# Output projection of the last block from single fp32 products to split halves (one Trainium2 core)

## The chip, the cores and the metric

One core of one Trainium2 chip runs the whole program. The metric is device time in microseconds (us) of one execution; lower is better. The time before is the median of three runs.

## The reference, cut to what matters

A two-layer first model (each layer: feed-forward, a mixing block, cross attention, feed-forward, each with a layer norm) is followed by one second-model block on 256 tokens of width 1024. The change is in that last block:

```python
y = sigmoid(ma) * ya + sigmoid(mb) * yb            # 256 x 1024, fp32
h = layer_norm_2(DEEPNORM_ALPHA * h + y @ w_out[i], ln1_g[i], ln1_b[i])
m = moe(h, w_router, b_router, w_up, b_up, w_down, b_down)   # 32 experts, top 4
h = layer_norm_2(DEEPNORM_ALPHA * h + m, ln2_g, ln2_b)
h = h + sigmoid(h @ w_ple_gate + b_ple_gate) * (p @ w_ple)
```

`ya` comes from a gated linear recurrence, `yb` from gated linear attention, normalised by the root of its mean square. `ma`, `mb` and the gates are projections of h. Only `y @ w_out` is computed in another way after the change.

## The kernel before, in words

**Weights.** SyncE (SP) loads weight tiles of 128 x 2048 fp32 (1 MB) into slots 0 to 5 of a ring of 12. A slot is free again when TensorE (PE) has counted the tile as used. Two forms of product exist. In the plain form PE multiplies fp32 by fp32; the trace then has two matmul records for one product. In the split form weight and activation are each the sum of two fp32r parts: high (ScalarE, ACT, copies with rounding, L1299 in `high`) and low (VectorE, DVE, subtracts, L1766 in `low`, written over the tile in its ring slot). PE then makes three fp32r products, high x high, high x low and low x high, one record each (`by_columns` L583 with 256 columns, `by_rows` L607, `rows_part` L596 and `tail` L645 with 512 columns). The high halves of weights take turns in ring slots 6 to 8; the halves of the activations lie in slots 9 (`xh`) and 10 (`xl`).

**Who splits when.** A list of tile names, `split_order` with `ORDER_MIX2` as its end, gives the order. `three_on(name)` is the tile three places later: `next_high(name)` on ACT (L1301) waits until `name` has been used by PE, which frees its high slot, and copies the tile three on; `next_low(name)` on DVE (L1769) subtracts for it. Where nothing is three on, neither does anything. Before the change the list ends with `ma3`, so the four tiles `w2o0` to `w2o3` of the output projection are not split.

**The end of the last block before the experts.** PE's order (L1002 on): `ga3`, `ma0`, `ma1` (split, by columns), sixteen matmuls with a matrix of ones for the mean squares (L1011, two banks, 0 and 1), then `ma2` in bank 0 and `ma3` in bank 1, then the output projection in the plain form: tile 0 for both halves t of the tokens, then tiles 1 to 3 for t = 0 and then for t = 1, with the eight transposes of the normed half t = 0 (L634) put before the last product group. ACT's order (L1651 on): sigmoid of `ma0`, `ma1` (L1643 in `through_r`, each followed by `next_high`), two square roots of the mean squares (L1405 in `roots`, they empty banks 0 and 1), sigmoids of `ma2` and `ma3`, a table load for the layer norm, the layer norm. DVE's order (L2154 on): low of `ma3`, gates `ma0`, `ma1` (L2132), two reciprocals (L2162), then for each j of 0 to 3 the part y_j: two products out of PSUM (L2166), one (L2173), for j of 2 and 3 the gate product (L2132), one addition (L2178). Then the layer norm (L1807).

**The experts.** Router, top 4, positions and gates follow the layer norm on PE, DVE and ACT (L1053 to L1089). SP starts to load expert 0 into all 12 slots as soon as `w2o3` is used (L541), as four pairs for the up projection and two pairs for the down projection; each later pair waits until PE has used the slots' former contents. Per expert PE gathers tokens (L1126), makes gate and up (L1154), transposes (L1167), combines (L1135) and makes the down product (L1192).

Of the kernel before, what the change touches and what calls it, by code (L numbers as in the profile page):

```python
# [16 lines left out]
F32 = mybir.dt.float32  # L17
F32R = mybir.dt.float32r
U8 = mybir.dt.uint8
ALU = mybir.AluOpType  # L20
# [3 lines left out]
P = 128  # L24
T = 256
TT = T // P
D = 1024
# [102 lines left out]
class Fork:  # L130
# [21 lines left out]
    def join(self):  # L152
        for ln, n in zip(self.lines, self.most):
# [3 lines left out]
ORDER_MIX1 = ("rq0", "rq1", "cc", "ch", "cb", "pu", "ri0", "ri1", "ck0", "ck1", "ck2", "ck3", "rg0", "rg1",  # L157
              "cv0", "cv1", "cv2", "cv3", "wo0", "wo1", "wo2", "wo3", "cq2", "cq3", "co0", "co1", "co2", "co3")
ORDER_MIX2 = ("xa2", "xa3", "q0", "q1", "k0", "k1", "v0", "v1", "v2", "v3", "go0", "go1", "go2", "go3",
              "mb0", "mb1", "mb2", "mb3", "ga0", "ga1", "ga2", "ga3", "ma0", "ma1", "ma2", "ma3")  # L160


def ffn_order(tag):
# [18 lines left out]
def program(nc, book, a):  # L182

    book.iters = {}
    with ExitStack() as ctx:
# [19 lines left out]
        hn = sb("hn", [P, TT, D])  # L205
# [20 lines left out]
        ps = ctx.enter_context(nc.psum_tensor("ps", [P, 8, 512], F32))  # L226
# [9 lines left out]
        dve_done = line("dve_done")  # L236
# [12 lines left out]
        slot_of = book.slots  # L249
# [15 lines left out]
        yT = w(Y, 2048, "p (g t) -> p g t", g=8)  # L265
# [3 lines left out]
        xh = ring_halves[XH][:].rearrange("p (k t) -> p k t", k=DT)  # L269
        xl = ring_halves[XL][:].rearrange("p (k t) -> p k t", k=DT)  # L270
# [287 lines left out]
        def _(pe):  # L558
# [5 lines left out]
            def open_bank(b, name):  # L564

                emptied[b].add(name)
                pe.wait_ge(emptied[b].sem, emptied[b].at(name))
# [4 lines left out]
            def arrived(name, plus=0):  # L572
                s = slot_of[name]
                pe.wait_ge(loaded[s].sem, loaded[s].at(name, plus))
                return s

            def release(mm, name):
                mm.then_inc(used[slot_of[name]].sem, 1)

            def full(mm, name):  # L580
                mm.then_inc(pe_full.add(name), 1)
# [46 lines left out]
            def transposes(tag, t, src):  # L628

                b = t_bank(tag, t)  # L630
                open_bank(b, ("T", tag, t))
                open_bank(b + 1, ("T", tag, t))
                for k in range(DT):
                    mm = pe.transpose(ps[:, b + k // 4, (k % 4) * P:(k % 4) * P + P], src[:, t, strip(tag, k)],  # L634
                                      ident[:])
                full(mm, ("T", tag, t))

            def normed(tag, t):
                pe.wait_ge(dve_done.sem, dve_done.at(("hn", tag, t)))
# [303 lines left out]
            s = arrived("glr")  # L943
            for k in range(DT):
                mm = pe.matmul(ps[0:16, 0, 0:T], ring[:, s, k * 16:k * 16 + 16], hT[:, k, :],
                               start=(k == 0), stop=(k == DT - 1))
# [25 lines left out]
            s = arrived("glg")  # L972
            for j in range(2):
                open_bank(2 + j, ("zg", j))
                for kk in range(2):
                    c0 = (2 * j + kk) * P
                    mm = pe.matmul(ps[:, 2 + j, kk * T:kk * T + T], ring[0:16, s, c0:c0 + P], work[0:16, FQ:FQ + T],
                                   start=True, stop=True)
# [35 lines left out]
            by_columns("ma2", 0)  # L1014
            by_columns("ma3", 1)

            def w2o_part(j, kk, t):
                s = slot_of[f"w2o{j}"]
                for half in range(2):
                    mm = pe.matmul(ps[:, 4 + 2 * t + half, :], yT[:, 2 * j + kk, t * P:t * P + P],  # L1020
                                   ring[:, s, kk * D + half * 512:kk * D + half * 512 + 512],
                                   start=(j == 0 and kk == 0), stop=(j == 3 and kk == 1))
                return mm

            def y_part(j):
                arrived(f"w2o{j}")
                pe.wait_ge(dve_done.sem, dve_done.at(("y", "g", j)))

            y_part(0)
            for t in range(TT):  # L1030
                open_bank(4 + 2 * t, "w2o")
                open_bank(5 + 2 * t, "w2o")
                for kk in range(2):
                    mm = w2o_part(0, kk, t)
            release(mm, "w2o0")
            after = ("A",)
            for j in (1, 2, 3):
                y_part(j)
                for kk in range(2):
                    mm = w2o_part(j, kk, 0)  # L1040
            full(mm, ("t0", after))
            for j in (1, 2, 3):
                for kk in range(2):
                    if (j, kk) == (3, 1):
                        normed(after, 0)
                        transposes(after, 0, hn)
                    mm = w2o_part(j, kk, 1)
                release(mm, f"w2o{j}")
            normed(after, 1)
            transposes(after, 1, hn)  # L1050
            turned_copied(after, 0)
# [226 lines left out]
        def _(act):  # L1278
# [50 lines left out]
            def root_table():  # L1329
                nc.scalar.activation(small[:, 61:62], epsc[:, 0:1], ACT.Sqrt)  # L1330
# [306 lines left out]
            def through_r(nm, j, fn):  # L1637
                slot_used(act, f"{nm}{j}")
                if j >= 2:
                    act.wait_ge(dve_done.sem, dve_done.at((nm, j - 2)))  # L1640
                elif nm == "ma":
                    act.wait_ge(dve_done.sem, dve_done.at(("ga", 2 + j)))
                nc.scalar.activation(work[:, R + 512 * (j % 2):R + 512 * (j % 2) + 512], ps[:, j % 2, :], fn)\  # L1643
                    .then_inc(emptied[j % 2].sem, 1)
                next_high(f"{nm}{j}")
# [7 lines left out]
            roots([("ms", "g", j) for j in range(2)], 256, 0)  # L1653
            through_r("ma", 2, ACT.Sigmoid)
            through_r("ma", 3, ACT.Sigmoid)
            root_table()
            ln(("A",), ("ln1_g_2", "ln1_b_2"), 0)

# [77 lines left out]
        def _(dve):  # L1736
# [3 lines left out]
            def done(ins, name):  # L1740
                ins.then_inc(dve_done.add(name), 1)
# [14 lines left out]
            def act_event(name):  # L1756
                dve.wait_ge(act_done.sem, act_done.at(name))
# [11 lines left out]
            def next_low(name):  # L1769
                ahead = three_on(name)  # L1770
                if ahead is not None:
                    low(ahead)
# [34 lines left out]
            def ln(tag, gname, i, alpha):  # L1807


                parts = tail_of(tag)  # L1810
                dve.wait_ge(h_ready.sem, h_ready.at(("h", before_ln(tag))))
                for t in range(TT):
                    if t == 0:
                        pe_group(("t0", tag))
                    else:
                        slot_used(dve, parts[2])
                    for half in range(2):
                        c = slice(half * 512, half * 512 + 512)
                        v.scalar_tensor_tensor(out=hn[:, t, c], in0=h[:, t, c], scalar=alpha,
                                               in1=ps[:, 4 + 2 * t + half, :], op0=ALU.mult, op1=ALU.add)\  # L1820
                            .then_inc(emptied[4 + 2 * t + half].sem, 1)
                    for half in range(2):
                        bank_empty(4 + 2 * t + half, acc_name(tag))
                        ins = v.bn_stats(stat[:, t, half, :], hn[:, t, half * 512:half * 512 + 512])
                    done(ins, ("stats", tag, t))
                    mine(("stats", tag, t))
                    normalise_rows(tag, t)
                    evac_T(tag, t, gname, i)
                    if tag[0] != "A":
                        x_low(tag, t)  # L1830
                if tag[0] != "A":
                    for name in parts:
                        next_low(name)
# [321 lines left out]
            for j in range(2):  # L2155
                mine(("ga", j))
                times("ma", j)

            dve.wait_ge(pool_done.sem, pool_done.at(("mb", 3)))
            for j in range(2):  # L2160
                bank_empty(j, ("ms", "g", j))
                link(v.reciprocal(work[:, Q + 512 * j:Q + 512 * j + 512], work[:, Q + 512 * j:Q + 512 * j + 512]))  # L2162
            for j in range(4):
                for uu in range(2):
                    u = 2 * j + uu
                    ins = v.scalar_tensor_tensor(out=work[:, FQ + u * T:FQ + u * T + T],  # L2166
                                                 in0=ps[:, obank("g", j), uu * T:uu * T + T],
                                                 scalar=col("gla_norm_g_2", uu), in1=work[:, Q + j * T:Q + j * T + T],
                                                 op0=ALU.mult, op1=ALU.mult)
                ins.then_inc(emptied[obank("g", j)].sem, 1)  # L2170
                bank_empty(obank("g", j), ("O", "g", j))
                x = work[:, FQ + 512 * j:FQ + 512 * j + 512]
                link(v.tensor_tensor(x, x, hn[:].rearrange("p t n -> p (t n)")[:, 512 * j:512 * j + 512], ALU.mult))  # L2173
                if j >= 2:
                    mine(("ga", j))
                    times("ma", j)
                mine(("ma", j))
                done(v.tensor_tensor(work[:, Y + 512 * j:Y + 512 * j + 512], x,  # L2178
                                     work[:, XC + 512 * j:XC + 512 * j + 512], ALU.add), ("y", "g", j))
            ln(("A",), ("ln1_g_2", "ln1_b_2"), 0, ALPHA2)  # L2180


# [304 lines left out]
```

## Time and profile before

| | |
|---|---|
| median of 3 runs | 2537.65 us (2536.61 to 2537.88) |
| the profiled execution's own time | 2539.67 us |
| its span, first to last instruction | 2537.9 us |
| PE busy | 2446.8 us (96%) |
| DVE busy | 1101.9 us (43%) |
| ACT busy | 827.2 us (33%) |
| POOL busy | 217.8 us (9%) |
| read from HBM | 662.50 MB, 261 GB/s over the span |
| mean granted TensorE clock | 0.982 |

All positions in the trace are microseconds from the first instruction. "Busy" adds up the time in which an engine has an instruction running. A timeline line is: start, duration, engine, line, operation, output <- inputs, how many were merged, and in brackets the idle time of the engine before it and what ended it. The end of a matmul is modelled and contains the way through the array, so the pace of a row of matmuls is read from start to start, not from the duration of one.

### The profile page before, as it was taken

What the parts mean: (1) busy time and instruction counts of PE and PEld (TensorE: products, weight loads), DVE (VectorE), ACT (ScalarE), POOL (GpSimd) and SP (SyncE); (2) the same over time, 40 slices, a digit from 0 to 9 for tenths busy, and PEclk for the clock granted to TensorE, in tenths of its full rate; (3) what the DMA queues carried; (4) which work ended last, traced back from release to release, by engine and by line L of the source; (5) the groups of instructions that cost most, each with busy time, mean ns of one, the idle gap of its engine ahead of it and who ended that gap; (6) DMA issues with size and microseconds to landing.
All of it is one profiled execution on the core that took longest, in us unless ns stands there. A gap on an engine that the chain in (4) does not pass through costs nothing. (4 is left out here: it accounts for less than half of the span.)

```text
span 2537.9 us, 36251 instructions
## 1 busy us (share of the span) xinstructions
PE 2446.8 (96%) x15029; PEld 1797.8 (71%) x15029; DVE 1101.9 (43%) x1411; ACT 827.2 (33%) x952; POOL 217.8 (9%) x101
## 2 busy tenths in 40 slices
PE   8999999999999999999999989999999999999977
PEld 8899988999999998899989944444444444444433
DVE  5457756644644867654569721112211111211122
ACT  4344344433433444443355411212221122212120
POOL 0002402200200432100111010000000000000001
PEclk9999999999999999999999979999999999999997
DMA  7565454565565545456455347999999999999980
GB/s 238 191 202 163 150 183 143 173 199 182 170 207 175 164 150 170 146 184 205 156 163 185 117 199 316 427 429 428 428 429 429 428 428 428 428 428 429 429 368 17
DMA packets 215307, 665.16 MB, mean 262 GB/s; under 512 B 9841, under 2 KB 164207, under 8 KB 190624
## 3 DMA queue, kind: packets, MB, share of 16 engines
q1 hardware_dynamic: 214912, 662.53, 68.4%
q8 instruction: 86, 1.41, 0.2%
q10 hardware_dynamic: 288, 1.05, 0.1%
q14 instruction: 21, 0.17, 0.0%
HBM read 662.50 MB, written 1.05 MB: 261 GB/s over the span
## 5 line engine op out<-in xcount | busy, mean ns | idle before, releaser
L592 PE MATMUL ps<-ring_halves 128*128 128x256 f32 x5984 | 757.4, 284 | 7.9 <-DVE ring_halves L1862 5.6
L592 PEld LDWEIGHTS ps<-ring_halves 128*128 128x128 f32 x5984 | 738.1, 193 | 12.0 <-DVE ring_halves L1862 6.0
L1766 DVE TENSOR_TENSOR ring_halves<-ring,ring_halves 128x2048 fp32r<-128x2048 f32 x206 | 516.0, 2513 | 367.7 <-ACT ring_halves L1299 367.5
L1299 ACT CAST ring_halves<-ring 128x2048 fp32r<-128x2048 f32 x206 | 391.3, 1903 | 280.9 <-PE ps L592 138.2
L1154 PE MATMUL ps<-ring,work 128*64 128x512 f32 x2048 | 452.8, 596 | 23.1 <-DMA ring<-in_w_up_dram 22.3
L1287 ACT COPY work<-ps 128x512 f32<-128x512 f32 x185 | 106.9, 587 | 844.8 <-PE ps L1154 391.5
L1154 PEld LDWEIGHTS ps<-ring,work 128*64 128x64 f32 x2048 | 145.8, 137 | 324.1 <-issue 269.4
L603 PE MATMUL ps<-ring_halves,work_halves 128*128 128x512 f32 x1184 | 288.5, 391 | 0.0
L2254 DVE TENSOR_SCALAR work<-work 128x128 f32<-128x128 f32 x64 | 19.3, 343 | 606.3 <-PE ps L1154 606.3
L2375 POOL TENSOR_TENSOR h<-hn,work 128x1024 f32<-128x1024 f32 x20 | 79.0, 3949 | 2106.8 <-DVE hn L1804 1066.9
L603 PEld LDWEIGHTS ps<-ring_halves,work_halves 128*128 128x128 f32 x1184 | 219.7, 188 | 44.4 <-issue 0.5
L1192 PE MATMUL ps<-ring,work 128*64 128x512 f32 x1024 | 226.8, 595 | 2.0
L1192 PEld LDWEIGHTS ps<-ring,work 128*64 128x64 f32 x1024 | 70.8, 137 | 137.5 <-issue 127.9
L603 PE MATMUL ps<-ring_halves 128*128 128x512 f32 x544 | 138.3, 393 | 1.3 <-ACT work L1287 1.3
L1126 PE MATMUL ps<-work,h 128*128 128x64 f32 x1056 | 132.8, 286 | 2.1 <-issue 2.1
L1126 PEld LDWEIGHTS ps<-work,h 128*128 128x128 f32 x1056 | 130.0, 200 | 3.6 <-issue 3.6
L673 PE MATMUL ps<-hT,ring 128*128 128x128 f32 x1024 | 118.1, 276 | 3.3 <-ACT hT L1317 3.3
L673 PEld LDWEIGHTS ps<-hT,ring 128*128 128x128 f32 x1024 | 116.2, 192 | 6.5 <-ACT hT L1317 6.5
L603 PEld LDWEIGHTS ps<-ring_halves 128*128 128x128 f32 x544 | 101.6, 188 | 23.6 <-issue 2.9
L2271 DVE TENSOR_TENSOR work<-work 128x256 f32<-128x256 f32 x64 | 27.2, 425 | 135.6 <-ACT work L1684 131.6
L1349 ACT ACTIVATE work<-ps 128x512 f32<-128x512 f32 x44 | 26.3, 597 | 140.2 <-PE ps L592 140.2
L1135 PE MATMUL ps<-work 64*128 64x512 f32 x264 | 65.6, 615 | 0.7 <-ACT work L1287 0.7
(260 smaller groups left out, 1744.3 us busy)
## 6 DMA issues: line engine op xcount, KB each, us to landing
ring<-in_w_up_dram SPq DMA_DIRECT2D x128, 2048.0 KB, 22.3
ring<-in_w_down_dram SPq DMA_DIRECT2D x64, 2048.0 KB, 19.4
ring<-in_w_in_dram SPq DMA_DIRECT2D x52, 1024.0 KB, 5.2
ring<-in_ffn_gate_dram SPq DMA_DIRECT2D x44, 1024.0 KB, 5.3
ring<-in_ffn_up_dram SPq DMA_DIRECT2D x44, 1024.0 KB, 5.3
ring<-in_ffn_down_dram SPq DMA_DIRECT2D x44, 1024.0 KB, 4.9
ring<-in_w_out_dram SPq DMA_DIRECT2D x12, 1024.0 KB, 4.9
ring<-in_ca_k_dram SPq DMA_DIRECT2D x8, 1024.0 KB, 5.1
```

The lines of the kernel that those rows point to most:

```text
L592: mm = pe.matmul(ps[:, bank, pt * T:pt * T + T], wt[:, o:o + P], x[:, k, :], start=(k == 0 and n == 0), stop=(k == DT - 1 and n == 2))
L603: mm = pe.matmul(ps[:, 4 + 2 * t + half, :], x, wt[:, o:o + 512], start=(start and n == 0), stop=(stop and n == 2))
L673: mm = pe.matmul(ps[:, bank, pt * T + t * P:pt * T + t * P + P], ring[:, slot_of[name], o:o + P], hT[:, k, t * P:t * P + P], start=(k == 0 ...
L1126: mm = pe.matmul(ps[:, 2, k * CAP:k * CAP + CAP], h[:, t, strip(("A",), k)], work[:, GS + t * CAP:GS + t * CAP + CAP], start=(t == 0), sto ...
L1135: mm = pe.matmul(ps[:, 4 + 2 * t + half, :], work[lo:lo + CAP, GGT + t * P:GGT + t * P + P], work[lo:lo + CAP, YS:YS + 512], start=False, ...
L1154: mm = pe.matmul(ps[lo:lo + CAP, x, :], work[:, XG + k * CAP:XG + k * CAP + CAP], ring[:, s, c0 + 512 * x:c0 + 512 * x + 512], start=(k == ...
L1192: mm = pe.matmul(ps[half * CAP:half * CAP + CAP, 3, :], work[:, ACTS + f * CAP:ACTS + f * CAP + CAP], ring[:, s, kk * D + half * 512:kk * ...
L1287: nc.scalar.copy(dst, ps[:, bank, :] if src is None else src).then_inc(emptied[bank].sem, 1)
L1299: nc.scalar.copy(high_of(name)[:], ring[:, s, :]).then_inc(hi_done.add(name), 1)
L1766: v.tensor_tensor(ring_halves[s][:], ring[:, s, :], high_of(name)[:].bitcast(F32), ALU.subtract)\
L2271: done(v.tensor_tensor(w(ACTS + 256 * x, 256), uh, w(SG + 256 * x, 256), ALU.mult), ("few", x))
L2375: link(g.tensor_tensor(h[:, t, :], hn[:, t, :], w(at, D), ALU.mult))
```

## The change

The names `w2o0` to `w2o3` are put at the end of the split list. That alone makes four existing calls do something they did not do: ACT's `next_high` behind the sigmoids of `ma1`, `ma2` and `ma3` now copies the high halves of `w2o0`, `w2o1` and `w2o2`. The copy behind `ma1` stands ahead of the two square roots in ACT's order. On DVE, `next_low` for `ma1`, `ma2` and `ma3` is called behind the parts y_1, y_2 and y_3. After the last sigmoid, ACT copies the four high parts of y into `xh` (which the gate projections have used until then), then the high half of `w2o3`, for which it waits until PE has used `w2o0`. DVE makes the four low parts of y behind the low half of `w2o2`, then the low half of `w2o3`. PE's hand-written projection is replaced by `by_rows` and `tail`, in the same order of tiles and token halves.

```diff
-              "mb0", "mb1", "mb2", "mb3", "ga0", "ga1", "ga2", "ga3", "ma0", "ma1", "ma2", "ma3")
+              "mb0", "mb1", "mb2", "mb3", "ga0", "ga1", "ga2", "ga3", "ma0", "ma1", "ma2", "ma3", "w2o0", "w2o1", "w2o2", "w2o3")
...
-            y_part(0)
-            for t in range(TT):
-                open_bank(4 + 2 * t, "w2o")
-                open_bank(5 + 2 * t, "w2o")
-                for kk in range(2):
-                    mm = w2o_part(0, kk, t)
-            release(mm, "w2o0")
+            def y_ready(j):
+                pe.wait_ge(dve_done.sem, dve_done.at(("ylow", "g", j)))
+
             after = ("A",)
-            for j in (1, 2, 3):
-                y_part(j)
-                for kk in range(2):
-                    mm = w2o_part(j, kk, 0)
-            full(mm, ("t0", after))
-            for j in (1, 2, 3):
-                for kk in range(2):
-                    if (j, kk) == (3, 1):
-                        normed(after, 0)
-                        transposes(after, 0, hn)
-                    mm = w2o_part(j, kk, 1)
-                release(mm, f"w2o{j}")
+            y_ready(0)
+            by_rows("w2o0", halves(0), start=True, opening="w2o")
+            tail(after, [(f"w2o{j}", halves(2 * j), lambda j=j: y_ready(j)) for j in (1, 2, 3)])
...
             through_r("ma", 2, ACT.Sigmoid)
             through_r("ma", 3, ACT.Sigmoid)
+            for j in range(4):
+                act.wait_ge(dve_done.sem, dve_done.at(("y", "g", j)))
+                done(nc.scalar.copy(xh[:, 2 * j:2 * j + 2, :], yT[:, 2 * j:2 * j + 2, :]), ("yhigh", "g", j))
+            next_high("w2o0")
             root_table()
...
+            def y_low(i):
+                act_event(("yhigh", "g", i))
+                done(v.tensor_tensor(xl[:, 2 * i:2 * i + 2, :], yT[:, 2 * i:2 * i + 2, :],
+                                     xh[:, 2 * i:2 * i + 2, :].bitcast(F32), ALU.subtract), ("ylow", "g", i))
...
                                      work[:, XC + 512 * j:XC + 512 * j + 512], ALU.add), ("y", "g", j))
+                if j:
+                    next_low(f"ma{j}")
+            for j in range(4):
+                y_low(j)
+            next_low("w2o0")
             ln(("A",), ("ln1_g_2", "ln1_b_2"), 0, ALPHA2)
```

## Rows read from the trace of the kernel before

**Rows 1.** The page, the span in 40 equal slices: bandwidth.
```profile
GB/s 238 191 202 163 150 183 143 173 199 182 170 207 175 164 150 170 146 184 205 156 163 185 117 199 316 427 429 428 428 429 429 428 428 428 428 428 429 429 368 17
```

**Rows 2.** Timeline of PE around the output projection.
```profile
1444.63 11.86 PE L592 MATMUL ps<-ring_halves 128*128 128x256 f32 x96
1459.50 27.68 PE L1020 MATMUL ps<-ring,work 128*128 128x512 f32 x60 [3.01 <-DVE work L2166]
1487.02 1.10 PE L634 MATMUL ps<-ident,hn 128*128 128x128 f32 x8
1487.96 1.88 PE L1020 MATMUL ps<-ring,work 128*128 128x512 f32 x4
```

**Rows 3.** Busy time, clock and DMA by stretch.
```profile
core 0: us, PE busy (x) PEld busy (x) DVE busy (x) ACT busy (x) POOL busy (x), PEclk, DMA share, GB/s
1456.50:1459.50 3.00, 0.00 (x1) 0.03 (x1) 2.90 (x6) 2.08 (x3) 0.00 (x0) 1.00 0.00 0
1459.50:1463.80 4.30, 4.30 (x6) 1.80 (x7) 1.96 (x3) 0.00 (x0) 0.00 (x0) 0.60 0.00 0
1489.80:1494.00 4.20, 0.04 (x1) 0.00 (x0) 3.67 (x7) 0.29 (x1) 0.00 (x0) 1.00 0.62 187
1494.00:1520.00 26.00, 20.99 (x68) 14.87 (x68) 5.43 (x30) 4.63 (x9) 4.69 (x2) 0.51 1.01 430
1529.30:1536.10 6.80, 6.80 (x18) 2.00 (x20) 0.00 (x0) 1.13 (x1) 0.00 (x0) 0.56 0.01 2
1700.00:2400.00 700.00, 678.20 (x3508) 299.02 (x3506) 128.39 (x384) 144.10 (x216) 0.00 (x0) 1.00 1.01 429
```

**Rows 4.** Timeline of SP, the loads of expert 1 into the up slots.
```profile
1536.13 10.63 SPq L370 DMA_DIRECT2D ring<-in_w_up_dram  x4
```

**Rows 5.** Timeline of PE, gate and up of expert 0 and expert 1.
```profile
1529.26 16.91 PE L1154 MATMUL ps<-ring,work 128*64 128x512 f32 x64 [0.75 <-ACT work L1287]
...
1560.40 13.90 PE L1154 MATMUL ps<-ring,work 128*64 128x512 f32 x64
```

**Rows 6.** Timeline of ACT ahead of the output projection.
```profile
1430.54 1.89 ACT L1299 CAST ring_halves<-ring 128x2048 fp32r<-128x2048 f32 x1
1432.45 1.28 ACT L1643 ACT_TABLE_LOAD   x1
...
1441.56 0.60 ACT L1643 ACTIVATE work<-ps 128x512 f32<-128x512 f32 x1 [3.37 <-PE ps L592]
1442.18 1.28 ACT L1405 ACT_TABLE_LOAD   x1
...
1443.47 0.69 ACT L1405 ACTIVATE work<-ps,epsc 128x512 f32<-128x512 f32 x1
```

**Rows 7.** Timeline of DVE ahead of the output projection, and the norm of its first half.
```profile
1432.46 2.29 DVE L1766 TENSOR_TENSOR ring_halves<-ring,ring_halves 128x2048 fp32r<-128x2048 f32 x1 [8.22 <-ACT ring_halves L1299]
1434.67 0.69 DVE L2132 TENSOR_TENSOR work<-work 128x512 f32<-128x512 f32 x1
...
1444.26 6.74 DVE L2162 RECIPROCAL work<-work 128x512 f32<-128x512 f32 x2 [1.31 <-ACT work L1405]
...
1451.04 0.87 DVE L2166 SCALAR_TENSOR_TENSOR work<-ps,cols,work 128x256 f32<-128x256 f32 x2
...
1460.84 0.69 DVE L2178 TENSOR_TENSOR work<-work 128x512 f32<-128x512 f32 x1
...
1482.00 0.81 DVE L1804 TENSOR_SCALAR hn<-hn,mv,rstd 128x1024 f32<-128x1024 f32 x1
```

**Rows 8.** Timeline of DVE in an earlier layer, the low half of 512 columns.
```profile
608.85 0.69 DVE L1847 TENSOR_TENSOR work_halves<-work,work_halves 128x512 fp32r<-128x512 f32 x1
```

**Rows 9.** Timeline of PE, 24 split products of 512 columns and what follows.
```profile
468.67 5.63 PE L603 MATMUL ps<-ring_halves,work_halves 128*128 128x512 f32 x24
474.13 11.68 PE L592 MATMUL ps<-ring_halves 128*128 128x256 f32 x96
```

**Rows 10.** Timeline of PE, 96 products of 256 columns after a longer idle time.
```profile
82.59 14.15 PE L592 MATMUL ps<-ring_halves 128*128 128x256 f32 x96 [5.61 <-DVE ring_halves L1862]
```

More of the change, by code:

```diff
@@ L1015, in _ @@
             by_columns("ma3", 1)
[L1017 to L1027, printed above, removed]
-            y_part(0)
-            for t in range(TT):
-                open_bank(4 + 2 * t, "w2o")
-                open_bank(5 + 2 * t, "w2o")
-                for kk in range(2):
-                    mm = w2o_part(0, kk, t)
-            release(mm, "w2o0")
-            after = ("A",)
-            for j in (1, 2, 3):
-                y_part(j)
-                for kk in range(2):
-                    mm = w2o_part(j, kk, 0)
-            full(mm, ("t0", after))
-            for j in (1, 2, 3):
-                for kk in range(2):
-                    if (j, kk) == (3, 1):
-                        normed(after, 0)
-                        transposes(after, 0, hn)
-                    mm = w2o_part(j, kk, 1)
-                release(mm, f"w2o{j}")
+            def y_ready(j):
+                pe.wait_ge(dve_done.sem, dve_done.at(("ylow", "g", j)))
+            after = ("A",)
+            y_ready(0)
+            by_rows("w2o0", halves(0), start=True, opening="w2o")
+            tail(after, [(f"w2o{j}", halves(2 * j), lambda j=j: y_ready(j)) for j in (1, 2, 3)])
             normed(after, 1)
```

## The prediction, made before the changed kernel was run

> **What bounds the kernel now.** I read the page's 40 slices first. From slice 25 on the bandwidth stands at 428 to 429 GB/s, while before that it wanders around 180 [rows 1]. So there are two regimes: PE sets the time up to the experts, and the experts run at the pace of their weight loads. The stretch table says the same: from 1700 to 2400 us the DMA share is 1.01, and PE has 22 us free in 700 [rows 3]. The reader has to see what joins the regimes. The twelve slots hold just one expert, and the loads of expert 1 start when PE has used the first pair of expert 0, at 1536.13 [rows 4], 6.9 us after its gate and up products began at 1529.26 [rows 5]. From there the stream is full, so the end of the kernel moves one to one with that moment, and that moment hangs on PE's chain through projection, layer norm and router. No slack in the experts absorbs a shift: a stream that starts later ends later.
>
> Next I read the timelines around the projection, one engine at a time. PE ends `ma3` at about 1456.5 and begins the projection at 1459.50, after 3.0 us of idle time; it ends at 1487.96 + 1.88 = 1489.84, so it takes 30.3 us [rows 2]. In those 3.0 us DVE is busy for 2.90 [rows 3]: from the reciprocals at 1444.26 to the last addition at 1460.84 DVE works without a break [rows 7]. PE is quick to be held up here because DVE is the engine that is late. That is what the change has to be weighed against: it relieves PE and adds work to DVE.
>
> **What it takes from PE.** The plain projection is 64 records, 30.3 us with its transposes. The new one has 4 tiles x 2 row blocks x 2 token halves x 2 column halves x 3 = 96 products. A block of 24 such products has its successor start 474.13 - 468.67 = 5.46 us after it, 0.2275 us each [rows 9]; 96 make 21.8 us. With the transposes at 1487.96 - 1487.02 = 0.9 us [rows 2] and 0.2 us for the way out of the last product this is 22.9 us at full clock. 30.3 - 22.9 = 7.4 us would be the gain if both ran under the same clock.
>
> They do not. After 3.0 us of idle time the clock was 0.60 of full in the first 4.3 us [rows 3], a loss of 1.7 us that lies within the 30.3. After an idle time of 5.61 us, 96 products took 14.15 us [rows 10], where 96 of the same kind at full clock took 11.86 [rows 2]: 2.3 us lost. The new idle time will be 12.8 us (below), for which no row stands; the bounds are 1.7 (the row after 3.0 us) and 3.4 (twice that), and I take 2.3, the row with the longer idle time. The new projection then takes 25.2 us, which is 5.1 less than now.
>
> The rows of plain products give another possible pace: 60 records from 1459.50 to 1487.02, less the 1.7 us, are 0.43 us each [rows 2, 3]. If a record is two passes, a pass of 512 columns takes 0.215 us, and 96 take 20.6 us, 1.2 us less than by rows 9. I keep rows 9, because they are the same instruction in the same helper. The Trainium skill (TensorE: Matmul & The Clock Gate, Back-to-back issue gap) gives 216 ns for an isolated product of 512 columns, by which the sum would be 1.1 us smaller. The same section gives some 131 ns for sustained pairs of weight load and product; that would be 12.6 us and turn the sum to a gain of about 3 us (estimates from the page). The trace disagrees with both, by its 0.2275 us.
>
> **What it puts on the path.** I follow it instruction by instruction.
>
> (a) ACT, behind the sigmoid of `ma1` at 1441.56: the copy of `w2o0` (slot free, tile landed) would start 0.5 us later and push the table load from 1442.18 to 1443.96, since a table load follows such a copy by 1432.45 - 1430.54 = 1.91 us. The square root moves from 1443.47 to 1445.25, by 1.8 us [rows 6]. Two things wait for it. PE wants bank 0 for `ma2`: it began at 1444.63 [rows 2] and now begins at about 1446.1, so `ma3` ends at 1457.9 instead of 1456.5; this 1.4 us hides behind (b). DVE wants the root: its chain moves from 1444.26 to 1446.0 [rows 7]. Only this second wait counts.
>
> (b) DVE, three low halves of weights between and behind the parts of y: each takes 2.29 us and holds the next instruction back by 1434.67 - 1432.46 = 2.21 [rows 7], so 6.6 us. Their high halves are done by then (copies behind the sigmoids of `ma1`, `ma2`, `ma3`, the last at about 1460.4, wanted at 1467.7). Nothing else runs on DVE that could cover them.
>
> (c) DVE, the low half of y_0: 0.69 us [rows 8]. The copies of y on ACT run while DVE works and cost nothing; if that cover were gone, the one in front of PE would cost another 0.6 us, the length of ACT's instruction on 512 columns [rows 6].
>
> So PE may start after the last addition, which lets a successor go at 1461.5 [rows 7], plus 1.8, plus 6.6, plus 0.7, plus 0.1 for the event: 1470.7 instead of 1459.5. **PE starts 11.2 us later**, after 12.8 us of idle time. It can't start on y_0 earlier, although y_0 is ready long before, because DVE makes all low parts behind y_3.
>
> (d) `w2o3`: its high half waits for PE to use `w2o0`, 24 products into the projection. Copy 1.9 and subtraction 2.3 with two events make 4.4 us; PE has the 24 products of `w2o1` and `w2o2` for t = 0 in the meantime, 5.5 us. It fits by 1.1 us, so 0.
>
> (e) Layer norm: the last product of t = 0 is PE's 40th record now, at about 1459.5 + 40 x 0.43 + 1.7 = 1478.4, and DVE has normed that half at 1482.00 + 0.81 = 1482.8 [rows 7], 4.4 us later; PE will have 30 products, 6.8 us, in that time, so 0. SP's order is unchanged; expert 0's loads start later with `w2o3`, need some 30 us and have as long as before. POOL does nothing here.
>
> **The sum.** 11.2 later, 5.1 shorter: +6.1 us at the layer norm, and through the router to 1536.13 unchanged in length. The clock there adds luck. Expert 0's first products had a clock of 0.56 [rows 3], and all 64 took 16.91 where expert 1's took 13.90 [rows 5]: 3.0 us are lost, and where the clock rises relative to the work can be better for the changed kernel by up to 1.7, or worse by a little. I take 0.2 off for it: +5.9. The working is in the profiled execution, which took 2539.67 us by its own time, 2.0 above the median; this execution would become 2545.6. Against the median of 2537.65 I forecast **2543.6 us**. About 0.2%, 5.1 us, is what a measurement can tell from no change.
>
> **The rivals.**
>
> *The shift stays under 5.1 us (within 0.2%), 0.27.* Either the root isn't pushed (table load or copy elsewhere in ACT's queue): then +4.1, 2541.8. Or the pace is 0.215: +4.7, 2542.4. Or the clock rises earlier at expert 0 than now: +4.2. For it speaks that the forecast lies only 0.8 us above the border; against the first that ACT runs in order in every row, against the second rows 9.
>
> *`w2o3` is late, or the clock stays low longer, 0.10.* The margin in (d) is 1.1 us, and the upper bound of the clock's loss costs 1.1 more than I took. A stall of 1 to 2 us on top makes +7 to +9, 2545 to 2547.
>
> *Faster: the clock stays up through the router, 0.04.* Place: the gap of 4.2 us after the projection. In it the clock was 1.00, and in the 26 us behind it 0.51, with PE busy for 21.0 [rows 3]. Should the clock stay at full there, at most half of the 21.0 would go, 10.5 us, and 3.0 at expert 0. It decides from 5.9 us saved; with all 13.5 the time is 2537.65 + 5.9 - 13.5 = 2530. Against it: the gap before and the waits within the stretch are as they were, and the change touches neither. The short pace of the page's sustained figure would end here too; it is counted in the 0.04.
>
> *The change doesn't do what it says* is no rival here: the four names enter the split list, and both engines' helpers follow that list.
>
> **How the numbers follow.** Forecast 0.59 with its own range of +5.1 to +7.3; under the border 0.27; later still 0.10; faster 0.04. For eight in ten I take +3.1 to +8.9: 2540.7 to 2546.5, which leaves out the faster case, the lowest tip of the second and the highest of the third. Slower by over 0.2%: 0.59 + 0.10 = 0.69; within: 0.27; faster: 0.04.
>
> **What would show it.** Right: root L1405 at about 1445.3; three subtractions L1766 of 2.29 us between 1457 and 1470; PE idle for 12 to 13 us before the first L603 product and reading DVE as its releaser; 96 products in 24 to 26 us with the transposes; SP's second batch of up loads at about 1542. Wrong: PE's first product before 1469 or after 1472, a gap on PE in front of `w2o3`, products at another pace than 0.2275 us, or a stretch from layer norm to experts that changes its length by over 2 us.

## The result, and the profile after

The changed kernel takes 2542.75 us (median of 16 runs, 2539.82 to 2546.17) against 2537.81 us before (16 runs, 2535.88 to 2541.45): 4.9 us more, ratio 1.002 with a 95% interval of 1.0012 to 1.0027, which is +3.0 to +6.9 us. The forecast was 2543.6 us, +5.9. Its profiled execution took 2543.03 us, span 2541.2.

The timeline of PE after, around the projection, the mean-square products (L1011) as its first row. Columns as in [rows 2].

```profile
1440.75 3.61 PE L1011 MATMUL ps<-work,ones 128*128 128x256 f32 x16
1445.38 11.77 PE L592 MATMUL ps<-ring_halves 128*128 128x256 f32 x96 [1.02 <-ACT work L1380]
1469.96 23.57 PE L603 MATMUL ps<-ring_halves 128*128 128x512 f32 x90 [12.81 <-DVE ring_halves L2140]
1493.38 1.11 PE L634 MATMUL ps<-ident,hn 128*128 128x128 f32 x8
1494.24 1.64 PE L603 MATMUL ps<-ring_halves 128*128 128x512 f32 x6
```

PE now waits 12.81 us where it waited 3.01 [rows 2], and its releaser is DVE's low part of y (L2140). A new, small gap of 1.02 us stands in front of `ma2` (second row), released by ACT's square root. The projection lasts from 1469.96 to 1495.88, 25.9 us, where it lasted 30.3.

The timeline of ACT after, which answers to [rows 6]:

```profile
1440.94 0.60 ACT L1618 ACTIVATE work<-ps 128x512 f32<-128x512 f32 x1 [3.37 <-PE ps L592]
1441.44 1.89 ACT L1274 CAST ring_halves<-ring 128x2048 fp32r<-128x2048 f32 x1
1443.35 1.28 ACT L1380 ACT_TABLE_LOAD   x1
1444.64 1.27 ACT L1380 ACTIVATE work<-ps,epsc 128x512 f32<-128x512 f32 x2
...
1478.61 1.91 ACT L1274 CAST ring_halves<-ring 128x2048 fp32r<-128x2048 f32 x1 [10.85 <-PE ps L603]
```

The copy stands between sigmoid and table load, and the root begins 3.70 us behind the sigmoid; before it was 1443.47 - 1441.56 = 1.91. The last row is the copy of `w2o3`, which waited for PE to use `w2o0`.

The timeline of DVE after, which answers to [rows 7]. The rows left out are instructions of y_0 to y_3.

```profile
1445.43 6.74 DVE L2146 RECIPROCAL work<-work 128x512 f32<-128x512 f32 x2 [3.09 <-ACT work L1380]
1452.20 0.88 DVE L2150 SCALAR_TENSOR_TENSOR work<-ps,cols,work 128x256 f32<-128x256 f32 x2
...
1456.69 2.28 DVE L1745 TENSOR_TENSOR ring_halves<-ring,ring_halves 128x2048 fp32r<-128x2048 f32 x1
...
1461.86 2.28 DVE L1745 TENSOR_TENSOR ring_halves<-ring,ring_halves 128x2048 fp32r<-128x2048 f32 x1
...
1466.41 0.69 DVE L2162 TENSOR_TENSOR work<-work 128x512 f32<-128x512 f32 x1
1467.02 2.28 DVE L1745 TENSOR_TENSOR ring_halves<-ring,ring_halves 128x2048 fp32r<-128x2048 f32 x1
1469.22 2.49 DVE L2140 TENSOR_TENSOR ring_halves<-work,ring_halves 128x512 fp32r<-128x512 f32 x4
1480.55 2.29 DVE L1745 TENSOR_TENSOR ring_halves<-ring,ring_halves 128x2048 fp32r<-128x2048 f32 x1 [8.84 <-ACT ring_halves L1274]
```

From 1445.43 to 1471.7 there is no idle time on DVE, with three low halves in between. The last row is the low half of `w2o3`: done at 1482.8. PE is busy for 19.88 of the 19.90 us in question (next fence), so it was in time.

Stretches of the kernel after, columns as in [rows 3]: the gap, the first 6 us of the projection, and the rest of it.

```profile
1457.20:1469.90 12.70, 0.00 (x0) 0.00 (x0) 12.50 (x15) 4.64 (x6) 0.00 (x0) 0.57 0.00 0
1470.00:1476.00 6.00, 6.00 (x14) 4.80 (x15) 1.71 (x3) 0.00 (x0) 0.00 (x0) 0.50 0.00 0
1476.00:1495.90 19.90, 19.88 (x91) 16.21 (x90) 7.33 (x12) 5.07 (x8) 4.73 (x2) 1.00 0.00 1
```

DVE is busy for 12.50 of the 12.70 us in which PE does nothing, and PE starts at a clock of 0.50.

SP after, the loads of expert 0 and the first of expert 1, which answers to [rows 4]:

```profile
1496.40 2.46 SPq L370 DMA_DIRECT2D ring<-in_w_up_dram  x4
...
1541.99 10.63 SPq L370 DMA_DIRECT2D ring<-in_w_up_dram  x4
```

**One ruler for all traces.** Executions differ by up to 2.5 us in what comes before. So the text below counts positions from the start of the mean-square products (L1011), whose operands the change doesn't touch; the fences keep the time from the first instruction. That start is at 1441.37 in the first trace of before and at 1440.75 after. The first output product comes at 18.1 before and 29.2 after, the load of expert 1 at 94.8 and 101.2.

### The profile page after: what moved, and what is told of

Its sections match the earlier page's. It is cut to its first block and busy times, and to the rows that moved or that the text cites. A ratio compares the mean times of both kernels' runs of the same rounds, so it can differ in the third digit from the quotient of the medians.

```text
span 2541.2 us, 36335 instructions
## 1 busy us (share of the span) xinstructions
PE 2441.4 (96%) x15061; PEld 1804.6 (71%) x15061; DVE 1113.5 (44%) x1419; ACT 836.7 (33%) x960; POOL 218.0 (9%) x101
## 5 line engine op out<-in xcount | busy, mean ns | idle before, releaser
L592 PEld LDWEIGHTS ps<-ring_halves 128*128 128x128 f32 x5984 | 737.8, 193 | 13.4 <-DVE ring_halves L1841 5.8
L1745 DVE TENSOR_TENSOR ring_halves<-ring,ring_halves 128x2048 fp32r<-128x2048 f32 x210 | 525.1, 2509 | 376.3 <-ACT ring_halves L1274 376.1
L1274 ACT CAST ring_halves<-ring 128x2048 fp32r<-128x2048 f32 x210 | 398.8, 1903 | 292.0 <-PE ps L592 138.2
L1129 PE MATMUL ps<-ring,work 128*64 128x512 f32 x2048 | 452.8, 596 | 23.1 <-DMA ring<-in_w_up_dram 22.3
L1129 PEld LDWEIGHTS ps<-ring,work 128*64 128x64 f32 x2048 | 145.6, 137 | 324.3 <-issue 269.4
L603 PE MATMUL ps<-ring_halves 128*128 128x512 f32 x640 | 163.5, 398 | 14.1 <-DVE ring_halves L2140 12.8
L603 PEld LDWEIGHTS ps<-ring_halves 128*128 128x128 f32 x640 | 121.7, 191 | 40.9 <-DVE ring_halves L2140 13.0
```

Source lines behind the costliest of these rows:

```text
L592: mm = pe.matmul(ps[:, bank, pt * T:pt * T + T], wt[:, o:o + P], x[:, k, :], start=(k == 0 and n == 0), stop=(k == DT - 1 and n == 2))
L603: mm = pe.matmul(ps[:, 4 + 2 * t + half, :], x, wt[:, o:o + 512], start=(start and n == 0), stop=(stop and n == 2))
L1129: mm = pe.matmul(ps[lo:lo + CAP, x, :], work[:, XG + k * CAP:XG + k * CAP + CAP], ring[:, s, c0 + 512 * x:c0 + 512 * x + 512], start=(k == ...
L1274: nc.scalar.copy(high_of(name)[:], ring[:, s, :]).then_inc(hi_done.add(name), 1)
L1745: v.tensor_tensor(ring_halves[s][:], ring[:, s, :], high_of(name)[:].bitcast(F32), ALU.subtract)\
```

## The experiments

The theory: PE's start is the end of DVE's chain, every low half on it costs its 2.2 us, ACT's early copy 1.8 us, and the products save what their pace says, less the clock. Rival A: PE waits for ACT's copies, not for DVE. Rival B: the loss is a matter of the clock and of luck behind the projection. The intervals below are those of the difference to the kernel before in runs on the same chip.

**1. ACT's roots first.**

```diff
-            def through_r(nm, j, fn):
+            def through_r(nm, j, fn, ahead=True):
...
-                next_high(f"{nm}{j}")
+                if ahead:
+                    next_high(f"{nm}{j}")
...
-            through_r("ma", 1, ACT.Sigmoid)
+            through_r("ma", 1, ACT.Sigmoid, ahead=False)
             roots([("ms", "g", j) for j in range(2)], 256, 0)
+            next_high("ma1")
```

> Edit: the changed kernel with one thing undone, the copy of w2o0's high half stands behind the two square roots on ACT. Theory (DVE's chain sets PE's start): roots, reciprocals and all that follows on DVE move 1.8 us earlier, PE's gate projections 1.4 us earlier, so PE's idle time before the first output product goes from 12.8 to about 12.4 us and the time falls by 1.8 us against the changed kernel (2542.75), to +3.1 against the kernel before. Rival A (PE waits for ACT's high halves, not for DVE): this puts the copy of w2o0 later by 2 us, PE starts later or no earlier, time +4.9 to +7. Rival B (the loss is phase of the clock and luck behind the projection): no change, +4.9.

```profile
1442.39 3.61 PE L1011 MATMUL ps<-work,ones 128*128 128x256 f32 x16
1445.65 11.86 PE L592 MATMUL ps<-ring_halves 128*128 128x256 f32 x96
1469.82 22.33 PE L603 MATMUL ps<-ring_halves 128*128 128x512 f32 x90 [12.31 <-DVE ring_halves L2142]
```

The fence is the PE timeline of this kernel. The gap before `ma2` is gone, the idle time is 12.31, and the first output product comes at 27.4, which is 1.8 earlier. The time is 2541.74 (11 runs) against 2538.01 of the kernel before on the same chip: +3.7, interval +0.5 to +5.1. Rival A wanted PE to start no earlier, and falls. Rival B wanted +4.9, which the interval of the runs doesn't exclude; this experiment leaves it to the next one.

**2. DVE's parts of y first.**

```diff
-                if j:
-                    next_low(f"ma{j}")
             for j in range(4):
                 y_low(j)
-            next_low("w2o0")
+                next_low(("ma1", "ma2", "ma3", "w2o0")[j])
```

> Edit: the changed kernel, with DVE's order changed only: all four parts of y first, then low of y_0, low of w2o0, low of y_1, low of w2o1 and so on. No work is removed. Theory: two lows of 2.2 us leave the path to PE's first product, idle time 12.8 - 4.4 = 8.4 us, time 4.4 us under the changed kernel, +0.5 against the kernel before. Rival A (ACT is what PE waits for): idle time stays 12.8, +4.9. Rival B (clock and luck): the idle time falls, but the time stays within 2 us of the changed kernel's.

```profile
1442.28 3.61 PE L1011 MATMUL ps<-work,ones 128*128 128x256 f32 x16
...
1467.14 22.16 PE L603 MATMUL ps<-ring_halves 128*128 128x512 f32 x90 [8.45 <-DVE ring_halves L1745]
```

In this PE timeline the start is at 24.9, 4.35 earlier, and the idle time is 8.45. The releaser is now L1745, the low half of `w2o0`. The same work in another order brings the time to 2536.85 (11 runs), -1.2 against before, interval -3.0 to +1.8: no difference that can be told. That is 6.1 under the changed kernel's +4.9, more than the theory's 4.4. At the load of expert 1 it is 6.2 earlier (94.65 against a mean of 100.86): 4.35 come from the start; 1.2 come from a projection of 24.5 us against 25.9 and 25.4, and 0.7 from behind the projection, both by an earlier rise of the clock (last section). Rival A wanted an idle time of 12.8 us and rival B a time within 2 us of the changed kernel's; both fall, though a part of the 6.1 is the clock.

**3. Both.** The two edits together.

> Edit: both of the former, ACT's roots first and DVE's parts first. Theory: the two add up, PE idle 12.4 - 4.4 = 8.0 us, 6.2 us under the changed kernel, -1.3 against the kernel before (2536.5). Rival B: within 2 us of the changed kernel.

The first output product comes at 23.1 (1464.67, mean-square products from 1441.59), 6.1 earlier than in the changed kernel; idle time 7.96. The time is 2538.06 (11 runs), 0.0 against before, interval -3.3 to +1.3. The start was as forecast; the total was forecast 1.3 lower, inside the interval.

**4. Low halves of the weights cut short.**

```diff
-                v.tensor_tensor(ring_halves[s][:], ring[:, s, :], high_of(name)[:].bitcast(F32), ALU.subtract)\
+                n = 8 if name in ("w2o0", "w2o1", "w2o2", "w2o3") else SLOT
+                v.tensor_tensor(ring_halves[s][:, 0:n], ring[:, s, 0:n], high_of(name)[:, 0:n].bitcast(F32), ALU.subtract)\
...
+                if name in ("w2o0", "w2o1", "w2o2", "w2o3"):
+                    low = high
```

> Edit: the changed kernel, with the low halves of the four w2o tiles cut to 8 of 2048 columns on DVE; PE multiplies by the high half once more in place of the low one, so the number and kind of its products is the same. Leaves out: the low half of w_out in the product, so the output is that of a rounded w_out. Theory: three subtractions of 2.2 us become about 0.1 us each, PE idle 12.8 - 6.3 = 6.5 us, 6.3 us under the changed kernel, -1.4 against the kernel before. Rival A (ACT): PE's start is then held by the last copy of y_0 or of w2o0 and moves by under 2 us. Rival B: within 2 us of the changed kernel.

The expectation is wrong on the output: the high product enters twice where the low one is missing, so the projection comes out far from that of a rounded `w_out`. The products on PE keep their number and kind. The three subtractions in front of PE's start last 0.16 us each. The first output product comes at 22.8 (1463.30, mean-square products from 1440.46), 6.4 earlier than in the changed kernel, after 6.43 us of idle time. The time is 2536.35 (11 runs), -1.7 against before, interval -3.8 to +0.8. So the three subtractions are 6.4 of the 11.1 us that PE starts late.

**5. PE kept busy in the gap.**

```diff
+            pe.wait_ge(emptied[6].sem, emptied[6].at("w2o"))
+            pe.wait_ge(pool_done.sem, pool_done.at(("mb", 3)))
+            for _ in range(12):
+                pe.matmul(ps[:, 6, :], ones[:], hn[:, 0, 0:512], start=True, stop=True)
             y_ready(0)
```

> Edit: the changed kernel, with 12 fp32 products of 512 columns (ones by the gated values, into a bank that the projection opens later and overwrites) put on PE between ma3 and the wait for y_0's low part. They take 10.3 us of the 12.8 us of idle time. Theory: they keep the clock at full, and the projection takes 23.0 us instead of 25.9 from first product to last; PE's start does not move; 2.9 us under the changed kernel, +2.0 against the kernel before. Rival (the 25.9 us are the products' own pace behind a wait, not the clock): the projection stays at 25.9 us and the time at +4.9.

```profile
1442.70 3.61 PE L1011 MATMUL ps<-work,ones 128*128 128x256 f32 x16
...
1458.95 10.46 PE L1024 MATMUL ps<-hn,ones 128*128 128x512 f32 x24
1471.93 20.70 PE L603 MATMUL ps<-ring_halves 128*128 128x512 f32 x90 [2.52 <-DVE ring_halves L2144]
1492.47 1.11 PE L634 MATMUL ps<-ident,hn 128*128 128x128 f32 x8
1493.33 1.64 PE L603 MATMUL ps<-ring_halves 128*128 128x512 f32 x6
```

In this PE timeline the start is at 29.2 as in the changed kernel, and the projection takes 23.04 us, from 1471.93 to 1494.97. The granted clock is 1.00 in the 2.52 us in front of it and all through it, so the clock had cost 25.92 - 23.04 = 2.9 us in the first trace of the changed kernel. The time is 2541.28 (11 runs) against 2537.34: +3.9, interval +2.3 to +6.9, more than the +2.0 expected and not to be told from the changed kernel's +4.9. So the rival is excluded by the trace (23.04 us, clock 1.00), not by the time. The load of expert 1 comes at 97.6, which is 3.0 after that of the kernel before (94.6, mean of three traces, below). The expectation was counted from the measured +4.9, while the traces put the changed kernel at +6.3 there (experiment 9); 6.3 less 2.9 would be 3.4.

**6. The kernel before, second token half first.**

```diff
             y_part(0)
-            for t in range(TT):
+            for t in (1, 0):
```

> Edit: the kernel before, with one thing changed, the plain projection's first tile goes through the second token half first (banks 6 and 7, free long before) and then the first (banks 4 and 5, which DVE empties with its last two parts of y). Theory: PE's 3.0 us wait was for bank 5 alone, y_0 is ready long before ma3 ends; PE goes on without a gap and the clock stays at full; 3.0 + 1.7 = 4.7 us under the kernel before, 2533.1. Rival (PE then waits for y_1 or for bank 5 a little later): a part of the 3.0 us comes back, 1.7 to 3 us under.

```profile
1442.51 3.61 PE L1011 MATMUL ps<-work,ones 128*128 128x256 f32 x16
1445.77 11.86 PE L592 MATMUL ps<-ring_halves 128*128 128x256 f32 x96
1457.47 25.91 PE L1020 MATMUL ps<-ring,work 128*128 128x512 f32 x60
```

The PE timeline has no bracket on the third row: PE goes on at once. Start at 15.0 instead of 18.1; the projection takes 28.6 us (to 1486.05) instead of 30.3, with a granted clock of 1.00 throughout, which bears out the 1.7 us that the prediction read for the clock. The time is 2532.25 (11 runs), -5.1, ratio 0.9979 (0.9970 to 0.9988). The wait of the kernel before was for PSUM, not for data, and its trace says for which bank. Bank 4 is emptied by y_2 and bank 5 by y_3. Here are DVE's products out of them in the kernel before:

```profile
1455.52 0.87 DVE L2166 SCALAR_TENSOR_TENSOR work<-ps,cols,work 128x256 f32<-128x256 f32 x2
...
1458.48 0.87 DVE L2166 SCALAR_TENSOR_TENSOR work<-ps,cols,work 128x256 f32<-128x256 f32 x2
```

Bank 4 was free at 1456.4, before `ma3` ended at 1456.5; bank 5 was free at 1459.35, and PE started at 1459.50. So it was bank 5 alone.

**7. Two tiles plain, two split.** On the changed kernel: `w2o0` and `w2o1` in the plain form, `w2o0` with token half 1 first, ACT's roots first, and on DVE

```diff
-            for j in range(4):
+            for n, j in enumerate((2, 3), 1):
                 y_low(j)
-            next_low("w2o0")
+                next_low(f"ma{n}")
```

> Edit: w2o0 and w2o1 in the plain form, token half 1 first for w2o0, only w2o2 and w2o3 split; ACT's copies behind the roots, DVE's low halves behind the last part of y (low y_2, low w2o2, low y_3, low w2o3). Theory: the plain products, 32 records at 0.43 us, cover the splitting on DVE (5.7 us from about 1461.5), PE has no gap and no low clock: 13.7 + 48 x 0.2275 + 1.1 = 25.7 us from 1456.6, end at 1482.3 against 1489.8 before, -7.5 us, 2530.3. Rival (DVE is late again): a gap in front of w2o2 or w2o3 of over 2 us and -5 or less.

```profile
1442.66 3.61 PE L1011 MATMUL ps<-work,ones 128*128 128x256 f32 x16
...
1457.62 10.46 PE L1034 MATMUL ps<-ring,work 128*128 128x512 f32 x24
1467.52 6.05 PE L603 MATMUL ps<-ring_halves 128*128 128x512 f32 x24
1473.41 3.59 PE L1034 MATMUL ps<-ring,work 128*128 128x512 f32 x8
1476.44 4.66 PE L603 MATMUL ps<-ring_halves 128*128 128x512 f32 x18
```

No row of this PE timeline has a wait. The projection ends at 1483.45, 40.8 on the ruler, where it ended at 48.5 before and at 43.5 in experiment 6. The time is 2529.88 (6 runs), -7.5, ratio 0.9969 (0.9957 to 0.9981).

**8. One tile plain, three split.** The same with `enumerate((1, 2, 3), 1)` and only `w2o0` plain.

> Edit: as the kernel with two split tiles, but w2o1 is split too, only w2o0 is plain. Theory: PE saves 16 x 0.43 - 24 x 0.2275 = 1.4 us, but reaches w2o1 at 1463.4, 1 us before DVE has its low half, and then goes at DVE's pace (2.9 us for each tile against 2.7 us); end at about 1482.2, the same -7.5 us within 1. Rival (split products are always worth it): -9.

```profile
1442.93 3.61 PE L1011 MATMUL ps<-work,ones 128*128 128x256 f32 x16
...
1457.89 7.03 PE L1034 MATMUL ps<-ring,work 128*128 128x512 f32 x16
1465.97 15.46 PE L603 MATMUL ps<-ring_halves 128*128 128x512 f32 x66 [1.04 <-DVE ring_halves L1779]
```

DVE is late by 1.04 us for `w2o1`, as expected. The projection ends at 1483.77, again 40.8 on the ruler. The time is 2529.07 (6 runs), -8.3, ratio 0.9967 (0.9955 to 0.9979). The two mixed kernels can't be told apart, so the rival's -9 isn't excluded by the runs; both beat both kernels of this study. Against experiment 6, which splits nothing and was run beside them, the medians are 2.4 and 3.2 us lower and the projection ends 2.7 us earlier. That is what the splitting itself gave; the other 5.1 us are the order of the token halves.

**9. The same kernels once more, to see what differs between executions of one kernel.** The first traces gave +6.5 us at the load of expert 1, but only +3.3 in the span.

> The kernel before once more, for its trace alone. In the first traces the changed kernel was 6.5 us late at SP's load of expert 1, and only 3.3 us late at the end; the difference lies behind the experts (PE without work for 8.0 us before the transposes of the last tokens in the kernel before, 6.3 in the changed one; 1.0 us in the last projection). Theory (luck of the execution: when instructions come and when the clock rises): the 8.0 and the length of the last projection differ between executions of the same kernel, and the distance from the mean-square products to the load of expert 1 stays at 94.8 within 1.7 us. Rival (the change shortens that stretch): it stays at 8.0 in every look at the kernel before.

> The changed kernel once more, for its trace alone. Theory: from the mean-square products to the first output product 29.2 us as in the first trace within 0.1 (it is DVE's chain), the projection 24.5 to 26.5 us depending on where the clock rises, the stretch behind the experts anywhere between 4.7 and 8 us. Rival (the change shortens that stretch): it stays at 6.3.

> As the first look at the kernel before. Theory: first output product 18.1 us behind the mean-square products within 0.1; the wait behind the experts different again. Rival: 8.0.

| | first output product | projection | load of expert 1 | PE idle behind the experts | span |
|---|---|---|---|---|---|
| before, first trace | 18.1 | 30.3 | 94.8 | 8.04 | 2537.9 |
| before, second trace | 18.1 | 30.3 | 94.5 | 6.48 | 2534.0 |
| before, third trace | 18.1 | 30.4 | 94.6 | 6.41 | 2534.8 |
| after, first trace | 29.2 | 25.9 | 101.2 | 6.29 | 2541.2 |
| after, second trace | 29.2 | 25.4 | 100.5 | 4.95 | 2542.1 |

Two rows of PE's timeline, of the first and of the second trace of before, show the largest step between two of them:

```profile
2470.42 1.09 PE L1251 MATMUL ps<-ident,ring 128*128 128x128 f32 x4 [8.04 <-issue]
```

```profile
2467.41 1.09 PE L1251 MATMUL ps<-ident,ring 128*128 128x128 f32 x4 [6.48 <-issue]
```

The rival, that the change shortens the stretch behind the experts, wanted 8.0 in every further trace of the kernel before and falls. The mean spans, 2541.7 (2 traces) and 2535.6 (3), differ by 6.1 us; the means at the load of expert 1 differ by 100.9 - 94.6 = 6.3.

## Why the prediction was right, by its own steps

**What bounds.** The shift goes through the experts: from the load of expert 1 to the same matmul group near their end (`L1154`, now `L1129`) it is 2447.74 - 1541.99 = 905.8 us after and 2441.66 - 1536.13 = 905.5 before. In the further traces it is 907.2 after, 905.3 and 905.9 before, so single traces differ there by up to 1.9 us. Over all kernels the time follows the position of that load, within 1.7 us (one trace each, three of before and two of the changed kernel):

| kernel | load of expert 1, against before (94.6) | time, against before |
|---|---|---|
| changed | +6.3 | +4.9 |
| roots first | +2.9 | +3.7 |
| parts first | +0.1 | -1.2 |
| both | 0.0 | 0.0 |
| short lows | -0.2 | -1.7 |
| kept busy | +3.0 | +3.9 |
| plain, half 1 first | -4.8 | -5.1 |
| two split | -9.2 | -7.5 |
| three split | -9.2 | -8.3 |

Of the -9.2 of the two mixed kernels, 7.7 lie before the end of the projection. The rest is the clock in the router and at expert 0: from the end of the projection to the load it is 44.6 us there and 45.3 to 46.3 in all other traces, and expert 0's 64 products take 15.8 us against 16.8 in experiment 6.

**(a) ACT's early copy.** Forecast 1.8 at the root and on DVE's chain; measured 3.70 - 1.91 = 1.79 at the root and 1.8 at PE's start (experiment 1). PE's new wait in front of `ma2` hid behind (b).

**(b) and (c) DVE.** Three low halves forecast at 6.6; taking nearly all of them away gave 6.4 (experiment 4), two of them moved gave 4.35 for 4.4 (experiment 2). The low half of y_0 began at 1469.22 and PE at 1469.96, 0.74 us for the 0.8 forecast. PE's start was forecast 11.2 later and came 29.2 - 18.1 = 11.1 later, after 12.81 us of idle time for 12.8.

**(d) and (e)** cost nothing, as forecast: no gap on PE before `w2o3` or the transposes.

**What PE saves.** At full clock 22.9 us were forecast and 23.04 measured (experiment 5). That settles the pace: 23.04 less the transposes' 0.9 and 0.2 for the way out is 21.9 for 96, 0.229 us each, by the block row and not by the 0.215 of a rival. The Trainium skill (TensorE: Matmul & The Clock Gate, Back-to-back issue gap) gives 216 ns for the isolated product and some 131 ns for sustained pairs. This trace agrees with neither; by the 131 ns (an estimate from the page) the sum would have been a gain.

**The clock** was the term with the widest bounds, 1.7 to 3.4, taken as 2.3. It measured 2.9 in the first trace and 25.4 - 23.0 = 2.4 in the second. That it lay near 2.3 is in part luck: after other idle times it was between 1.5 and 2.6 (last section), and not in the order that the prediction's choice of "the row with the longer idle time" assumes. Expert 0's products took 16.79 us where they had taken 16.91 [rows 5], so the 0.2 taken off for luck there was 0.1.

The sum by the traces is 11.1 - (30.3 - 25.7) - 0.2 = +6.3 at the load of expert 1, where 5.9 was forecast; the runs say +4.9, with an interval of +3.0 to +6.9 that holds both. Whether the change costs more or less than 5.1 us, the border of the chances, the runs leave open. Their median of +4.9 lies just under it, outside the forecast's own +5.1 to +7.3 and in the band of the first rival (0.27), though inside the eight-in-ten range. Of that rival's three mechanisms the first two did not occur: the root was pushed by 1.79 us and the pace was 0.229. The third, the clock at expert 0, gave 0.1. So the mechanism was right, and the mean of the traces lies 0.4 above the forecast; the runs' median is 1.4 under the traces' +6.3, which lies within its interval, and nothing here explains it.

**The rivals.** That the root isn't pushed and that `w2o3` is late are excluded by the rows above. That the clock stays up through the router is excluded too: from the end of the projection to the load of expert 1 it is 46.1 us after and 46.3 before, at a granted clock of 0.50 to 0.53 from the last transposes to expert 0 in both.

## What to carry to other kernels

Before an engine's work is made cheaper, ask which engine it waited for, and whether the cheaper form gives that one more to do: here PE won 5 us and lost 11 because the splitting stood in the chain of DVE, which was late already. The same splitting in another order was neutral. It paid once the plain products of the first tile or two covered it: 7.5 to 8.3 us under the kernel before. But 5.1 of these came from the order of the token halves alone, by which PE no longer waited for one PSUM bank; the splitting gave the other 2.4 to 3.2. A wait's releaser should be looked up before the work behind it is rebuilt.

## What the runs showed of the hardware that was not expected

The clock's price did not grow with the idle time. The loss of the split projection (its length less the 23.04 us at full clock) was 2.9 and 2.4 us after 12.8 us of idle time, 1.6 after 12.3 (projection 24.7, experiment 1), 1.5 after 8.45 (24.5, experiment 2), 2.6 after 7.96 (25.6, experiment 3) and 2.6 after 6.43 (25.6, experiment 4). The rows of the granted clock show where the loss comes from. In all six traces the clock stood at 0.50, the lower level of 1.2 GHz, in the last microsecond before PE's start. It was back at 1.00 some 6.2 and 5.2, 3.5, 3.1, 5.5 and 5.5 us after that start, in the same order (estimates from stretches of 1 us each). The loss is close to half of that time. So it goes by how late the clock rises, not by how long PE stood; what sets that moment was not tried. In experiment 5, where PE stood for only 2.52 us, the clock stayed at 1.00.

Behind the experts PE stands for 4.7 to 8.0 us before the transposes of the last tokens, with nothing in the profile that it waits for ("issue"), and differently in executions of the same kernel (8.04, 6.48 and 6.41; 6.29 and 4.95). So it accounts for 1.6 us between three traces of the kernel before, whose 16 runs scatter over 5.6 us. What it is was not tried.
